# A mixture of experts planned by load: several 64-row items on one load of weights

## The reference

```python
scores = jax.nn.sigmoid((t @ router_w).astype(jnp.float32))
sel = scores + router_b.astype(jnp.float32)
grouped = sel.reshape(-1, N_EXPERT_GROUPS, EXPERTS_PER_GROUP)   # 4 groups of 4
group_score = lax.top_k(grouped, TOP_K)[0].sum(-1)
g_idx = jnp.argmax(group_score, axis=-1)                        # one group per token
_, local = lax.top_k(in_group, TOP_K)                           # 2 experts of it
...
def expert(acc, p):
    wg, wu, wd, gate_col = p
    y = (jax.nn.silu(t @ wg) * (t @ wu)) @ wd                   # 1024x512, 1024x512, 512x1024
    return acc + gate_col[:, None] * y, None
```

## Time and profile before

| | |
|---|---|
| time, median of 3 runs | 2538.96 us (2538.04 to 2539.06) |
| span of the profiled execution | 2543.0 us |
| TensorE busy | 2310.8 us (91%) |
| feed-forward gate and up stage of the first block | 590.8 to about 755 us |
| expert items, first layer | 1524.1 to 1853.5 us: 16 home items, 4 overflow items of 128 rows |
| expert items, second layer | 2248.7 to 2514.9 us: 16 and 2 items of 64 rows |

### The profile page before, as it was taken

One profiled execution on the slowest core, in us unless ns is written; L12 is line 12 of the kernel. 1 busy time (PEld: TensorE's weight loads), 2 busy tenths in 40 slices (PEclk: granted clock), 3 DMA queues, 4 the chain that ended last, 5 costly groups with the idle time before them and its releaser, 6 DMA issues. The chain is left out here.

```text
span 2543.0 us, 32710 instructions
## 1 busy us (share of the span) xinstructions
PE 2310.8 (91%) x13425; PEld 1594.8 (63%) x13425; DVE 989.5 (39%) x2060; ACT 504.9 (20%) x966; POOL 74.6 (3%) x79
## 2 busy tenths in 40 slices
PE   7999988898999799999768979998969999889996
PEld 6887887787888644455764445554447567745553
DVE  1366244312110469994666131110040565233333
ACT  0132511100100210014311020000031766121111
POOL 0000022002000000000000010000010000000000
PEclk9999999998999899999888989999969999989998
DMA  8443365247544322656002239999842212579995
GB/s 258 134 147 116 117 199 166 67 149 281 161 166 149 100 66 77 201 186 195 4 1 116 83 144 397 409 403 414 321 143 66 88 63 84 217 307 394 392 396 205
DMA packets 238131, 482.15 MB, mean 190 GB/s; under 512 B 13042, under 2 KB 192292, under 8 KB 208676
## 3 DMA queue, kind: packets, MB, share of 16 engines
q1 hardware_dynamic: 218304, 439.36, 48.2%
q0 software_dynamic: 6480, 23.60, 2.4%
q10 hardware_dynamic: 13204, 17.19, 2.1%
HBM read 453.36 MB, written 26.74 MB: 189 GB/s over the span
## 5 line engine op out<-in xcount | busy, mean ns | idle before, releaser
L1997 PE MATMUL bank<-hn,weights 128*128 128x512 f32 x640 | 279.9, 598 | 2.3 <-ACT hn L410 2.3
L1997 PEld LDWEIGHTS bank<-hn,weights 128*128 128x128 f32 x640 | 121.6, 191 | 152.8 <-issue 151.8
L2074 DVE SCALAR_TENSOR_TENSOR conv_sum<-mixer_then_weights_ahead,vec,conv_sum 128x572 f32<-128x572 f32 x240 | 174.8, 805 | 0.0
L578 PE MATMUL bank<-u,weights 128*128 128x256 f32 x768 | 170.8, 379 | 0.9 <-PEq L194 0.9
L3614 PE MATMUL bank<-hn,weights 128*128 128x512 f32 (+1 forms) x512 | 169.2, 488 | 0.0
L578 PEld LDWEIGHTS bank<-u,weights 128*128 128x128 f32 x768 | 144.8, 190 | 24.1 <-issue 5.4
L1591 PE MATMUL bank<-u,weights 128*128 128x256 f32 x704 | 155.3, 383 | 0.9 <-DVE u L391 0.9
L1591 PEld LDWEIGHTS bank<-u,weights 128*128 128x128 f32 x704 | 135.0, 192 | 19.8 <-issue 1.1
L3614 PEld LDWEIGHTS bank<-hn,weights 128*128 128x128 f32 x512 | 96.0, 190 | 65.3 <-issue 58.4
L3765 DVE SCALAR_TENSOR_TENSOR x_both<-bank,mod_later,x_both 128x256 f32<-128x256 f32 x144 | 63.1, 480 | 162.9 <-PE bank L2840 160.8
L2462 PE MATMUL bank<-mixer_then_weights_ahead,weights 128*128 128x512 f32 x256 | 111.8, 597 | 0.0
(11 more groups left out here) (578 smaller groups left out, 3305.4 us busy)
## 6 DMA issues: line engine op xcount, KB each, us to landing
weights<-in_mod_w SPq DMA_DIRECT2D x48, 1024.0 KB, 7.8
weights<-in_w_in SPq DMA_DIRECT2D x36, 1024.0 KB, 5.2
weights<-in_moe_w_gate SPq DMA_DIRECT2D x36, 1024.0 KB, 18.6
weights<-in_moe_w_up SPq DMA_DIRECT2D x36, 1024.0 KB, 19.2
weights<-in_moe_w_down SPq DMA_DIRECT2D x36, 1024.0 KB, 17.0
weights<-in_ab_w_in SPq DMA_DIRECT2D x20, 1024.0 KB, 5.4
mixer_then_weights_ahead<-in_moe_w_gate SPq DMA_DIRECT2D x20, 1024.0 KB, 23.3
mixer_then_weights_ahead<-in_moe_w_up SPq DMA_DIRECT2D x20, 1024.0 KB, 24.0
```

The costliest lines, as they stand in the source:

```text
L578: last = pe.matmul(bank(n), unit[:, k, m * P:(m + 1) * P], x(k), start=k == 0, stop=k == ktiles - 1)
L1997: last = pe.matmul(tile_bank(n)[:, :], unit[:, k, lane * P:(lane + 1) * P], hn[:, k, :], start=k == 0, stop=k == DC - 1)
L2074: ins = dve.scalar_tensor_tensor(s, x, w, s, ALU.mult, ALU.add)
```

## The change

1. A plan for each layer (`SlotPlan`) has 16 slots. Slots 0 to 2 are experts 0 to 2. The 13 others are ranked by load on VectorE (`rank_slots`); the plan says which rank stands in which slot and how many 64-row items it gets: in the first layer 4, 3 and 3 for ranks 0, 1 and 2 (slots 5, 9 and 13), in the second 2 and 2 for ranks 0 and 1 (slots 5 and 10), 1 for all others. Items of one slot use one load of weights. That makes 22 items that are written out in the first layer, 17 in the second; the 16th slot and whatever a plan leaves over go through a loop. On the loads above nothing is left over, so the loop runs once: 23 and 18 items, and 16 loads of weights in each layer. No item has 128 rows.
2. The ring frees a unit when the last item of its slot has used it. SyncE and ScalarE read the expert's number from a table into a register (`value_load`) for each slot of 3 to 14.
3. Order on TensorE: an item's four `gate_up`s come first, in the order gate, gate, up, up; after the second the next item's rows are turned, after the third the former item's hidden is turned, and after the fourth comes the former item's `down`. `xg` and the gate and up banks are doubled. Only items 0 and 1 are gathered by products; all others are loaded from `token_rows`.
4. In the second layer the scatter is two items behind, and item 15's scatter stands alone behind the last written-out item.
5. Each expert has a region of 8 * 64 rows in `token_rows`: 8192 rows, before 3200. The row of a token is its place plus 512 times the expert, so `route` has a shorter tail. The 25 zeroing DMAs become 64.
6. `list_overflow` (some 28 small VectorE operations) replaces `overflow_table`, behind item 1 instead of item 3.

```diff
-MOST_ROWS = EXPERTS * CAP + (ITEMS - EXPERTS + 1) * OVER
+REGION = 8
+MOST_ROWS = EXPERTS * REGION * CAP
...
+SLOT_PLANS = (SlotPlan((3, 4, 0, 5, 6, 7, 1, 8, 9, 10, 2, 11, 12), (1, 1, 4, 1, 1, 1, 3, 1, 1, 1, 3, 1, 1)),
+              SlotPlan((2, 3, 0, 4, 5, 6, 7, 1, 8, 9, 10, 11, 12), (1, 1, 2, 1, 1, 1, 1, 2, 1, 1, 1, 1, 1)))
...
+    def program(self, sp, inp, layer, table, slots_ready, table_ready, unit_done, over_used):
+        e = FIXED - 1
+        for u in range(self.size, self.units):
+            s, j = divmod(u, SLOTS)
+            if j == 0:
+                if s == FIXED:
+                    sp.wait_ge(slots_ready, 1)
+                e = slot_expert_of(sp, table, s)
+            freed_slot, freed = divmod(u - self.size, SLOTS)
+            sp.wait_ge(unit_done[freed], self.plan.last[freed_slot] + 1)
+            self.load(sp, u, expert_unit(inp, layer, e, j))
...
                 gather(0)
-                turn_gathered(0)
-                for at in range(EXPERTS):
-                    pe.wait_ge(x_copied, at + 1)
+                turn_rows(0)
+                for n, (slot, k) in enumerate(plan.item):
+                    pe.wait_ge(x_copied, n + 1)
                     for j in range(4):
-                        gate_up(at, j)
-                    if by_products(at + 1):
-                        gather(at + 1)
-                    if at + 1 < EXPERTS:
-                        turn_gathered(at + 1)
...
-                    pe.wait_ge(h_copied, at + 1)
-                    for j in range(2):
-                        down(at, j)
...
+                        release = over_used if slot == EXPERTS - 2 and j == 0 else None
+                        gate_up(n % 2, j, unit_of(n, j), unit_done[j], release)
+                        if j == 0 and n + 1 < BY_PRODUCTS:
+                            gather(n + 1)
+                        if j == 1:
+                            turn_rows(n + 1)
+                        if j == 2 and n >= 1:
+                            turn_hidden(n - 1)
+                    if n >= 1:
+                        down_static(n - 1)
+                turn_hidden(S - 1)
+                down_static(S - 1)
...
+                copy_gathered(0)
+                copy_turned(0, 0)
+                for n in range(S):
+                    if n + 1 < BY_PRODUCTS:
+                        copy_gathered(n + 1)
+                    copy_turned(n + 1, (n + 1) % 2)
+                    if n + 2 == BY_PRODUCTS:
                         act.wait_ge(rows_written, 16 * 2 * NT)
+                    if n + 2 < S:
+                        load_item(n + 2)
...
+                    silu(n, n % 2, (unit_done[1], n + 1))
+                    if n >= 1:
+                        store_item(n - 1)
```

More of the change, by code:

```diff
@@ L2552, in route @@
         chosen = new("chosen", NT, 16)
[L2553 to L2556, removed]
+        home = new("home_row", NT, 16)
+        weights, places, totals, key, part, high, low = share
         flat = lambda ap: ap.rearrange("p a b -> p (a b)")
@@ L2651, in _ @@
                 v = Signal(vsem)
[L2652 to L2656, removed]
@@ L2699, in experts @@
 def experts(kit, T, table, share, tokens, add, inp, layer, places_of, ahead, spare):
     nc = kit.nc
-    feed = kit.feed
     NT = T // P
     HALF, FOURTH = D // 2, DC // 2
-    UNITS, RING = EXPERTS * SLOTS, SLOTS + AHEAD
-    assert UNITS % RING == 0
-    weights, places, start, upto, _, _, _ = share
-    most = EXPERTS + max(1, (CHOICES * T - 1) // CAP)
-    assert most <= ITEMS
+    plan = SLOT_PLANS[layer]
+    S, b_loop = plan.static, plan.static % 2
+    RANKS = len(plan.item) - FIXED + 1
@@ new lines, in down @@
+                def down(n, b, j, unit, done):
+                    if j == 0:
+                        pe.wait_ge(turned_copied, n + 1)
+                    ht = turned[b][:, 0:256].rearrange("p (b a s) -> p b a s", b=2, a=2)
+                    for q in range(2):
+                        for ab in range(2):
+                            last = pe.matmul(y_bank[lane(ab), :], ht[:, q, j, :], unit.rearrange("p (k n) -> p k n", k=2)[:, q, ab * HALF:(ab + 1) * HALF],
+                                             start=j == 0 and q == 0, stop=j == 1 and q == 1)
+                    last.then_inc(done, 1)
@@ new lines, in _ @@
+                    if n >= 1:
+                        down_static(n - 1)
+                turn_hidden(S - 1)
+                down_static(S - 1)
+                count = loop_count(pe)
+                with pe.Fori(0, count) as i:
+                    n = i + S
+                    pe.wait_ge(x_copied, n + 1)
+                    for j in range(4):
+                        gate_up(b_loop, j, ring.loop_arrived(pe, i, j), over_used)
+                    turn_rows(n + 1)
+                    turn_hidden(n)
+                    pe.wait_ge(y_copied, n)
+                    for j in range(2):
+                        down(n, b_loop, j, ring.loop_arrived(pe, i, 4 + j), over_used)
@@ new lines, in _ @@
+                store_item(S - 1)
+                count = loop_count(act)
+                with act.Fori(0, count) as i:
+                    n = i + S
+                    silu(n, b_loop, (over_used, i * SLOTS + (SLOTS + 2)))
+                    copy_turned(n + 1, b_loop)
+                    load_rows(loop_block(i + 2))
+                    store_rows(n, b_loop, loop_block(i))
+                for b in range(2):
+                    stored = sum(32 for n in range(S) if n % 2 == b)
+                    act.wait_ge(y_stored[b], count * 32 + stored if b == b_loop else stored)
```

951 lines of the change are left out of this document (499 added, 452 removed).

## The result

The changed kernel takes 2522.95 us (median of 4 runs, 2518.89 to 2524.41), the kernel before 2538.53; the ratio is 0.993 (95% interval 0.9916 to 0.9944), so 0.6 to 0.8% faster. The forecast was 2509 with a range of 2484 to 2532. On a second chip the two took 2523.51 and 2541.37 us, ratio 0.9935 (0.9917 to 0.9953).

The account below looks back on a forecast made before the run. Weight loads and products were nearly level in the first expert stage; products bound the second. First layer -53.2, second +4.0, zeroing +19.5 gave -29.7: span 2513.3, less 4.0 for the median, 2509 us, range 2484 to 2532.

Parts of the forecast that it names:

- the step from the span to the time: Whole kernel: the median was taken as 4.0 us below the span, so span 2513.3 became 2509 us.
- Zeroing: First block's feed-forward stage: 64 zeroing DMAs take turns from the weights, so TensorE waits; +19.5 us, bounds 0 and 30.
- An item: First layer's expert stage: one 64-row item takes 11.65 us instead of 12.21, bounds 11.4 and 12.21.
- The rival of 12.21: First layer: drains or late signals eat the saved wait, an item keeps 12.21 us; +12, 2521 us, chance 0.15.
- Items 0 to 2: First layer's first items: item 0 takes 11.4 us, and item 2's rows come late, a 3.5 us wait (bounds 0 and 6).
- Weights: First layer's items: TensorE waits 1 us for weights instead of 13.0, bounds 0 and 8.
- Start: First layer's router: a shorter tail on VectorE, 2.0 us instead of 3.37, lets the first item start 1.4 us earlier.
- End: First layer's last items: item 21's hidden and down alone take 4.9 us, the loop's item 12.2.
- Stores and the way back of the rows stay as they are.: Behind the first layer's items: storing results and fetching rows back was forecast to change by 0 us.
- Second layer: Second expert stage: products bound, 14.75 us an item instead of 14.61; +4.0 us from an earlier start, bounds 0 and +9.
- zeroing hidden: Rival, feed-forward stage: the additional zeroing costs nothing; -49.2 us, 2490 us, chance 0.16.
- rows late: Rival, first layer: row loads land too late for 21 items, slower than before; +52, 2561 us at 12.7 us landings, chance 0.09.

Follow-up runs that it names:

- before_z64: The kernel before with 64 zeroing DMAs instead of 25, nothing else changed: 2561.64 us, 20.3 more than the kernel before in the same session (ratio 1.0079).
- z_1k: The changed kernel with its 33.6 MB of zeros in DMAs of 256 columns, meant as 1 KB pieces: 2506.14 us (one run).
- own_down2: The changed kernel with the old order within first-layer items (own hidden, then own down) and ScalarE's silu ahead of row copy and loads: 2521.6 us (one run).
- hold: The changed kernel, loading the next stage's first weights only after the last item's results are back from token_rows: 2520.21 us (one run).
- ones: The changed kernel with one item for each first-layer slot and the rest in the loop, 23 loads of weights instead of 16: 2615.09 us.
- early: The changed kernel with the first layer's slot of four items one place earlier, slot 4 instead of 5: 2527.25 us (one run).
- own_down: The changed kernel with the old order within first-layer items, but ScalarE's silu behind the row copy and two DMA issues: 2618.05 us.

## Why the forecast was right, and where it was off

The sign and the range held: 2522.95 lies 14 us above the forecast, 9 below the range's end. The two large mechanisms held as well, the zeroing that takes the weights' turns and the single load for several items. Three steps did not: the way back of the rows, the order counted as a saving of its own, and the step from the span to the time.

- **Zeroing.** +19.5 forecast, +20.2 in the trace, +20.3 alone (before_z64). The step was sound in its rate (89 GB/s), in the wait near 649 (13.7 forecast, 14.32), in the clock (2.4, 2.1) and in the end of the zeroing (692, some 695). That the sum came out so near is in part luck. The wait of 2.9 near 683 didn't come, only 0.5 did. In its place stands one of 2.7 near 633 that the sum hadn't: it kept the landing at 634.1 of the earlier trace rows although it says itself that the end of the zeroing had saved that unit, and without that end it lands at 635.7, when TensorE has wanted it since 633. The rule that each engine takes queues in turn, a packet each (the Trainium skill, DMA: Bandwidth & Descriptors, Queues, rings and completion order) agrees with 1417 packets to 1416 here. z_1k was meant to test what follows from it, that long packets take the bytes, and didn't.
- **An item.** 11.65 forecast, 11.76 measured (+2.2 us over 21). The rival of 12.21 falls for the order of after, and is just what own_down2 takes. But the sum of "21 items by what each saves" hid that the order's saving is paid elsewhere: the wait for item 2's rows was in the sum, as a term of its own, and never set against the order alone.
- **Items 0 to 2.** Item 0 11.2 (11.4), wait for rows 3.49 (3.5). Missing from the term: the products behind the wait run at the lower clock until item 2 starts (granted 0.73 from 1557 to 1567.5 us), (1567.58 - 1549.68) - 11.75 - 3.49 = 2.7 us. I had counted this for the zeroing and forgot it here.
- **Weights.** 1 us forecast, 3.2 measured, inside the bound of 8.
- **Start.** The first gather comes 1.5 us earlier, as forecast, by the shorter tail; the gather then runs at a lower clock (6.26 us, 5.50 before), and 0.8 is left.
- **End.** 4.8 (4.9), the loop's item 12.4 (12.2).
- **"Stores and the way back of the rows stay as they are."** This step failed: +3.7 us. In before the next stage's weights are issued from 1833.80 on, and from 1854.5 to 1866 us, the store and the way back, no weights are on the queues. In after they are issued from 1798.63 on, and from 1820 to 1830 us, beside the store, q1 moves 2.74 MB of them. hold takes them away and 3.2 of the 3.7 us with them.
- **Second layer.** 14.75 an item as forecast; the stretch +2.65 instead of +5.2. Of the 2.55 that are missing, 1.5 is the forecast wait for item 2's rows, which didn't come in this trace; the rest is in item 0, the lone scatter and the loop's item (9.5, 10.0 and 16.1 us instead of 9.8, 10.3 and 16.6). In twelve traces with the new code the stretch took 277.8 to 281.1, in two with the old code 275.2 and 277.0: longer in each pair, but by 0.8 to 5.9. Part of this is the clock at its start. In the six traces of 279.2 the first 16 products take 3.3 to 3.4 us, in the four of 277.8 they take 1.95.
- **A gain nobody forecast.** Behind the feed-forward stage 3.0 us came back, in before_z64 too. 2.6 of them lie in the first 131 us behind it, half of these in one stage: its 128 products take 30.91 us in the trace of before, 29.63 in that of after, with the same waits of some 6.4 us ahead.

```profile
845.03 30.91 PE L540 MATMUL bank<-loaded_rows_then_z_gates,weights 128*128 128x256 f32 x128 [6.39 <-PEq L194]
```

```profile
862.79 29.63 PE L575 MATMUL bank<-loaded_rows_then_z_gates,weights 128*128 128x256 f32 x128 [6.38 <-PEq L229]
```

  The granted clock was 0.79 in the first 15 us of it before, 0.87 in the first 14.2 after. Why the slow phase falls otherwise isn't shown. Nor does the gain belong to the zeroing for certain: the stretch takes 732.3 to 732.4 us in six of the nine traces with the wait near 650, but 735.5 to 735.7 in three others with the same wait (ones, early, hold), and 734.8 to 736.0 in all that are without it.

These terms make 3.7 us of the miss of 14 (span 2517.0, forecast 2513.3). That this is so little is luck in part: the stretches that came out longer than forecast do so by 12.4 us together, those that came out shorter by 8.8, and 5.1 of the 8.8 lie ahead of and behind the feed-forward stage, in stretches for which nothing was forecast. The other 10 are the step from span to median. In every later run the time is the span plus 1.8 or 1.9 us; I took "the median is 4.0 below the span" for a property of the kernel, when the traced execution of before was simply one of some 2545 us, 6 above its median, and the trace of after is of the fastest of its four (2518.89, median 2522.95). The sum of terms predicts a difference between two traces; how far both traces lie from their medians adds its own error, here 6.4 and 4.1 us together, two thirds of the measured gain of 15.6. What an untraced run does with its 4 us more stays open.

The rivals: zeroing hidden falls (before_z64); rows late falls, with at most 0.7 us for any item from 3 on in the nine traces with this order and plan or nearly; the plan does what it says, one loop item.

## What to carry to other kernels

A bulk write is not free because its queue has nobody waiting: count the packets per turn against a stage that lives from its loads, and put it where the DMA row of the page is near zero (20 us here, more than the whole measured gain). A software pipeline's saving per round must be set against what it moves forward at the start and in the prefetch, which is best seen by undoing the order alone. And before a sum is turned into a time, find out which execution the trace is of.

## What the hardware showed that I had not expected

- A wait of 2 to 4 us cost half to three quarters as much again in clock: 2.4 us of waiting in each item cost 4.2 (own_down), 3.5 us 5.4 (ones, 17.15 less 11.76), 3.49 us once 6.2. The shorter waits of 1.60 us (hold) and 1.76 (item 5 in after) had products at full speed behind them.
- GpSimd issues a DMA from a 128-partition tile in 0.53 us whether it has 512 or 128 KB (13.34 us for 25 in the earlier trace rows, 60.21 for 113 in z_1k), so pieces of 128 KB held its queue to 246 GB/s.
- HBM to HBM copies of 4 KB rows wrote 20.4 MB in some 65 us, 0.32 TB/s of zeros, each byte also read.
